# Linear attention: compact decayed queries, and a PSUM bank of level products per head instead of per pair of heads

## The chip, the cores and the metric

The kernel runs on one core of one Trainium2 chip. The metric is the device time of one execution in microseconds (us). Three runs of the kernel before gave a median of 2939.26 us (2933.54 to 2946.39).

## What is computed

The reference is one layer of a streaming encoder over two inputs, a prompt of 2048 tokens and 64 new tokens of a running stream, both 1024 wide. One projection feeds three groups of heads: gated linear attention (4 heads, keys of 64, values of 128), stick-breaking attention (4 heads of 64) and a short gated convolution. Their joined output is projected, added and normed, and a feed-forward part with squared ReLU follows. The change is in the gated linear attention alone, which works in chunks of 64 tokens:

```
b = cumsum(lg)                                   # per head and key channel
att[t, s] = sum_k q[t,k] * k[s,k] * exp(b[t,k] - b[s,k])     for s <= t
o = (q * exp(b)) @ S + att @ v
S = exp(b_last) * S + (k * exp(b_last - b))^T @ v
```

## The kernel before

The program has three phases, each closed by a barrier of all engines: `phase_in` (the input norm, the projection, the convolution), `phase_gla` (the gated linear attention) and `phase_tail` (stick-breaking attention, output projection, feed-forward). The change touches only `phase_gla`.

**Tiling.** Tokens come in four groups of 512 and one of 64 (`GG`), groups in tiles of 128, tiles in chunks of 64. The four heads lie as two pairs: a tile of queries or keys has 128 partitions, where partitions 0 to 63 are the 64 channels of a pair's first head and 64 to 127 those of its second, and an axis of 2 for the pair.

**Levels.** The decay between two tokens of a tile is computed without large exponents, by halving: on a level with half size hs (32, 16, 8, 4, 2, 1) each block of 2·hs tokens is cut in the middle. Keys of the first half are multiplied with the decay up to the cut (L1040), queries of the second half with the decay from the cut on (L1046), and a product of the two gives the attention of later on earlier halves. `level_arg` (VectorE, L1030 and L1031) writes the two exponents' arguments into a buffer `ex` of three slots, ScalarE takes the exponent (L943), `level_mul` (VectorE) multiplies with keys (in place, in `ex`) and queries (into `qb`, which holds only the 256 queries of second halves out of 512 tokens), `level_product` (TensorE, L1143) multiplies the two into the PSUM tile `ps_l`, two banks of 512 columns, and `level_put` copies the valid blocks into `att`: on ScalarE for levels 0 and 1 (L956, one instruction for each block of rows), on VectorE with a mask for levels 2 to 5 (L1074). A seventh step, the diagonal (`li == NL`), multiplies plain keys and queries of one token and head (L1150), with operands of 64 partitions, a bank for each head of the pairs, two tiles at a time.

**Queries with zeros.** Before, `qb` has an axis for the head: `qb[P, EX, 2, 2, 256]`, slot, pair, head, query. The first head's queries stand in partitions 0 to 63 of the first part, the second head's in partitions 64 to 127 of the second; the rest was zeroed once by GpSimd. So one product of all 128 partitions gives both heads of a pair side by side: 128 weight columns (the tile's keys) against 2 x 64 queries, four products (tiles) for each of two banks, one bank per pair. A float32 product shows in the trace as two records of matmul and two of weight load, so a level has 16 records of each.

**Around the levels.** For each tile: `intra` (att times values, L1189), `inter` (queries times state, L1210) and `state` (VectorE, L1093) for each of its chunks, `squares`, `root` and `norm` (the output's norm: ScalarE L972, TensorE L1220, ScalarE L980 and L982, VectorE L1104 and L1107), and for the next tile `turn` (keys turned by TensorE, L1161, copied by ScalarE, L965) and `kv` (L1176).

**Order.** A Python list `order` holds all steps; each engine walks through it and does its part, with semaphores between engines. The steps of group g+1's levels (`ahead`) are spread by weights over the tile steps of group g, from the fourth place on; the first group's stand before everything. Within a group the steps follow as: argument of level li+1, multiplication of level li, copy of level li-1, product of level li. These waits matter:

- a product waits for its level's multiplications (`lev_mul`), and for each bank until the level before has been copied out of that bank;
- a copy waits for the product's end in its own bank (`lev_mm`), so the first bank can be copied while the second is computed;
- the argument of level li waits until the product of level li-3 has read its slot of `ex`;
- `intra` waits for all copies of its group.

SP issues the loads and stores of the phase, and no DMA is changed. ScalarE and VectorE wait at the start for the memsets (`consts_set`): eps and the state on VectorE, `att` on VectorE (L988), `qs` and `qb` on GpSimd (L1225, L1226).

Of the kernel before, what the change touches and what calls it, by code (L numbers as in the profile page):

```python
# [20 lines left out]
P = 128  # L21
# [662 lines left out]
def phase_gla(nc, a, zt_dram, gv_dram, mixt_dram, lasting):  # L684
# [8 lines left out]
    with s:  # L693
# [11 lines left out]
        att = s.sb("att", [P, 2, 2, 4, 2, P])  # L705
        eb = s.sb("eb", [P, 2, 2, 512])

        qb = s.sb("qb", [P, EX, 2, 2, 256])
        qs = s.sb("qs", [P, 2, 2, 2, 512])
        ksf = s.sb("ksf", [P, 2, 2, 512])  # L710
        gg = s.sb("gg", [P, 2, 4, 512])
# [190 lines left out]
        def _(act):  # L902
# [2 lines left out]
                act.dma_start(bg[:], a["b_gate"][0].rearrange("(a p) -> p a", p=P)).then_inc(gate_in, 16)  # L905
            for dst, src in ((starts[:], a["chunk_start"][:, :512]), (masks[:], a["level_masks"]), (ident[:], a["ident"]), (ones[:], a["ones"])):
                act.dma_start(dst, src).then_inc(consts_in, 16)
            act.wait_ge(consts_set, 5)
            act.wait_ge(gate_in, 48)
            for step, *at in order:  # L910
                if step == "gate":
# [11 lines left out]
                elif step == "gate_log":  # L923
                    g = at[0]
                    n = GG[g][1]
                    act.wait_ge(gate_abs, g + 1)
                    act.activation(ga[:, :, :n], ga[:, :, :n], ACT.Exp, scale=-1.0).then_inc(gate_exp, 1)
                    act.wait_ge(gate_exp, g + 1)
                    act.activation(ga[:, :, :n], ga[:, :, :n], ACT.Ln, bias=1.0).then_inc(gate_ln, 1)
                elif step == "gate_sum":  # L930
                    g = at[0]
                    n, q = GG[g][1], g % 2
                    act.wait_ge(cum_done, 2 * (g + 1))
                    if g >= 2:
                        act.wait_ge(st_new, tiles[tiles_before[g - 1]][3][0])
                    act.activation(eb[:, q, :, :n], bc[:, q, :, :n], ACT.Exp, scale=1.0 / TAU).then_inc(eb_done, 1)
                    act.wait_ge(ks_arg, g + 1)
                    act.activation(ksf[:, q, :, :n], ksf[:, q, :, :n], ACT.Exp, scale=1.0 / TAU).then_inc(ks_exp, 1)
                elif step == "level_arg" and at[1] < NL:
                    g, li = at  # L940
                    n, x = GG[g][1], lev_no[(g, li)]
                    act.wait_ge(lev_arg, 2 * (x - g + 1))
                    act.activation(ex[:, x % EX, :, :n], ex[:, x % EX, :, :n], ACT.Exp, scale=1.0 / TAU).then_inc(lev_exp, 1)  # L943
                elif step == "level_put" and at[1] < BY_ROWS:
                    g, li = at
                    n = GG[g][1]
                    b, w, nt, hs = bank_no[(g, li, 0)], min(P, n), max(1, n // P), LEVELS[li]
                    wo = w // 2
                    if g >= 2 and li == 0:
                        act.wait_ge(o_mm, tiles_before[g - 1])  # L950
                    for e in range(2):
                        act.wait_ge(lev_mm, 2 * b + e + 1)
                        dst = att[:, g % 2, e, :nt, :, :w].rearrange("p a h t -> p (a h) t")
                        for x in range(w // (2 * hs)):
                            rows = slice(2 * hs * x, 2 * hs * x + hs)
                            put = act.activation(dst[rows, :, 2 * hs * x + hs:2 * hs * x + 2 * hs],  # L956
                                                 ps_l[rows, e, :2 * nt * wo].rearrange("p (x t) -> p x t", x=2 * nt)[:, :, hs * x:hs * x + hs], ACT.Copy)
                        put.then_inc(put_a, 1)
                elif step == "turn":
                    j = at[0]  # L960
                    m = tiles[j][2]
                    act.wait_ge(k_turned, j + 1)
                    if j >= 2:
                        act.wait_ge(kv_mm, tiles[j - 2][3][-1] + 1)
                    act.activation(kt[:m, j % 2, :], ps_k[:m, 0:256], ACT.Copy).then_inc(k_out, 1)  # L965
                elif step == "squares":
                    j = at[0]
                    m = tiles[j][2]
                    act.wait_ge(o_mm, j + 1)
                    if j:  # L970
                        act.wait_ge(n_mm, j)
                    act.activation(sq[:, :4 * m], ps_o[:, j % 2, :4 * m], ACT.Square).then_inc(sq_done, 1)  # L972
                elif step == "root":

                    j = at[0]
                    m = tiles[j][2]
                    act.wait_ge(n_mm, j + 1)
                    if j:
                        act.wait_ge(o_norm, j)
                    act.activation(rn[:, :4 * m], ps_g[:, :4 * m], ACT.Ln, scale=QSCALE * QSCALE / DV, bias=eps[:, :]).then_inc(n_ln, 1)  # L980
                    act.wait_ge(n_ln, j + 1)
                    act.activation(rn[:, :4 * m], rn[:, :4 * m], ACT.Exp, scale=-0.5).then_inc(n_exp, 1)  # L982

        @block.vector
        def _(dve):
            dve.memset(eps[:], LN_EPS).then_inc(consts_set, 1)
            dve.memset(st[:, 0, :, :], 0.0).then_inc(consts_set, 1)
            dve.memset(att[:], 0.0).then_inc(consts_set, 1)  # L988
            dve.wait_ge(consts_in, 64)
            for step, *at in order:  # L990
                if step == "gate_sum":
                    g = at[0]
# [15 lines left out]
                elif step == "decay":  # L1008
# [3 lines left out]
                    if g >= 2:  # L1012
                        dve.wait_ge(o_mm, tiles_before[g - 1])
                    dve.wait_ge(group_in[q], 48 * (g // 2 + 1))
                    dve.wait_ge(consts_set, 5)
                    for e in range(2):
                        r = slice(64 * e, 64 * e + 64)
                        dve.tensor_tensor(qs[r, q, :, e, :n], eb[r, q, :, :n], gq[r, q, :, :n], ALU.mult).then_inc(qs_done, 1)
# [13 lines left out]
                elif step == "level_mul" and at[1] < NL:  # L1032
# [5 lines left out]
                    k1, _ = halves(gk[:, q], g, hs, n)  # L1038
                    _, q2 = halves(gq[:, q], g, hs, n)
                    dve.tensor_tensor(e1, e1, k1, ALU.mult).then_inc(lev_mul, 1)  # L1040
                    dve.wait_ge(consts_set, 5)
                    if x >= EX:
                        dve.wait_ge(lev_mm, last_bank[lev_by_no[x - EX]])
                    for e in range(2):
                        r = slice(64 * e, 64 * e + 64)
                        dve.tensor_tensor(qb[r, x % EX, :, e, :n // 2].rearrange("p a (b h) -> p a b h", h=hs), e2[r], q2[r], ALU.mult).then_inc(lev_mul, 1)  # L1046
                elif step == "level_put" and at[1] >= BY_ROWS:

                    g, li = at
# [3 lines left out]
                    for (lj, ts) in level_blocks(g):  # L1053
# [3 lines left out]
                        for e in range(2):  # L1057
# [2 lines left out]
                                dve.wait_ge(lev_put, put_no[2 * b - 1][1])  # L1060
                            if li < NL:

                                dst = att[:w, g % 2, e, ts[0]:ts[0] + nt, :, :w].rearrange("p a h t -> p (a h) t")
                                hs, wo = LEVELS[li], w // 2
                                nb = w // (2 * hs)
                                for_pairs = dst.rearrange("p x (b two h) -> p x b two h", two=2, h=hs)[:, :, :, 1, :]
                                data = ps_l[:w, e, :2 * nt * wo].rearrange("p (x b h) -> p x b h", x=2 * nt, h=hs)
                                mk = masks[:w, 64 * li:64 * li + wo].bitcast(I32).rearrange("p (b h) -> p b h", h=hs).unsqueeze(1).to_broadcast([w, 2 * nt, nb, hs])
                            else:

                                for_pairs = att[:w, g % 2, :, ts[0]:ts[0] + nt, e, :w]
                                data = ps_l[:w, e, :2 * nt * w].rearrange("p (x a t) -> p x a t", x=2, a=nt)
                                mk = masks[:w, 64 * NL:64 * NL + w].bitcast(I32).unsqueeze(1).unsqueeze(1).to_broadcast([w, 2, nt, w])
                            dve.copy_predicated(for_pairs, mk, data).then_inc(lev_put, 1)  # L1074
                elif step == "state":
# [2 lines left out]
                    g, i, m, cs = tiles[ct]  # L1078
                    q, end = g % 2, i * P + x * CHUNK + CHUNK - 1
                    dve.wait_ge(kv_mm, c + 1)  # L1080
                    dve.wait_ge(consts_set, 5)
                    if c == FIRST_STREAM:
                        dve.wait_ge(st_in, 16)
                    if c:
# [25 lines left out]
        def _(pe):  # L1110
            pe.wait_ge(gate_in, 48)
            gates_seen = tiles_seen = 0
            for step, *at in order:
# [11 lines left out]
                elif step == "level_product":  # L1125
# [1 line left out]
                    x = lev_no[(g, li)]  # L1127
                    w = min(P, GG[g][1])
                    if li < NL:
                        pe.wait_ge(lev_mul, 3 * (x - g + 1))  # L1130
                    for (lj, ts) in level_blocks(g):
                        if lj != li:
                            continue
# [1 line left out]
                        for e in range(2):  # L1135
                            if b:
                                pe.wait_ge(*put_no[2 * b - 2 + e])
                            for n, t in enumerate(ts):
                                cols = slice(t * P, t * P + w)
                                if li < NL:  # L1140

                                    wo = w // 2
                                    mm = pe.matmul(ps_l[:w, e, n * w:n * w + w], ex[:, x % EX, e, cols], qb[:, x % EX, e, :, t * wo:t * wo + wo],  # L1143
                                                   start=n == 0, stop=n == len(ts) - 1, skip_group_check=True)
                                    continue

                                r = slice(64 * e, 64 * e + 64)
                                for pr in range(2):
                                    at_ = (pr * len(ts) + n) * w
                                    mm = pe.matmul(ps_l[:w, e, at_:at_ + w], gk[r, g % 2, pr, cols], gq[r, g % 2, pr, cols],  # L1150
# [44 lines left out]
                elif step == "inter":  # L1195
# [8 lines left out]
                    elif c:  # L1204
                        pe.wait_ge(st_new, c)
                    else:
                        pe.wait_ge(consts_set, 5)
                    cols = slice(i * P + x * CHUNK, i * P + x * CHUNK + CHUNK)
                    for pr in range(2):
                        mm = pe.matmul(ps_o[:, j % 2, 2 * m * pr:2 * m * pr + 2 * m].rearrange("p (e t) -> p e t", e=2)[:, :, x * CHUNK:x * CHUNK + CHUNK],  # L1210
# [11 lines left out]

        @block.gpsimd
        def _(pool):
            pool.memset(qs[:], 0.0).then_inc(consts_set, 1)  # L1225
            pool.memset(qb[:], 0.0).then_inc(consts_set, 1)  # L1226


def phase_tail(nc, a, zt_dram, mixt_dram, xn_dram, ks_dram, vs_dram, wd_dram, wp_dram, y_tile, lasting):
# [1107 lines left out]
```

## Time and profile before

| | |
|---|---|
| median of three runs | 2939.26 us (2933.54 to 2946.39) |
| profiled execution, its own time | 2947.04 us |
| its span in the trace | 2945.2 us |
| TensorE busy in the span | 2634.0 us, 89% |
| VectorE busy | 1711.7 us, 58% |
| ScalarE busy | 932.2 us, 32% |
| GpSimd busy | 620.3 us, 21% |
| linear attention phase in the span | 654 to 926 us |

The profile is one execution, written down by the chip's profiler. "PE" is TensorE's matmul, "PEld" its weight load, DVE is VectorE, ACT is ScalarE, POOL is GpSimd; SP issues DMAs. L1143 is line 1143 of the kernel. Busy time is the union of an engine's instructions; matmuls are pipelined, so a group's busy time is not the sum of its durations, and a record's duration is longer than the distance to the next. PEclk is the granted clock of TensorE as a share of 2.4 GHz. In a timeline, equal neighbours of one engine are merged (xN), and the bracket tells how long the engine had been idle and what released it.

### The profile page before, as it was taken

The page shows a single profiled execution, that of the slowest core. Times are in us where ns is not written, and L with a number is a line of the kernel's source. Part 1 is how long each engine was busy: PE and PEld are TensorE (multiplying, and loading weights), DVE is VectorE, ACT ScalarE, POOL GpSimd, SP SyncE. Part 2 cuts the span into 40 slices and gives each one's busy share as a digit, 9 for nine tenths or more (in the row PEclk, how much of TensorE's full clock was granted, in tenths as well). Part 3 has the DMA queues.
Part 4 walks back from the last instruction along what each step waited for, and adds up shares of the span by engine and source line. Part 5 has one row for each costly group of instructions (what it writes and reads, how often), then busy time and mean ns, then how long its engine had stood idle before and what let it go on. Part 6 is the DMA issues. An engine that isn't in the chain of part 4 may idle for free.

```text
span 2945.2 us, 37243 instructions
## 1 busy us (share of the span) xinstructions
PE 2634.0 (89%) x13462; PEld 2195.1 (75%) x13462; DVE 1711.7 (58%) x2482; ACT 932.2 (32%) x1816; POOL 620.3 (21%) x617
## 2 busy tenths in 40 slices
PE   6999999975774779999899999989999979999996
PEld 4887777973553568887687878868788767898985
DVE  6676667437784666666566555646656435533334
ACT  3333333313433434443413333322333220221220
POOL 4888788830000110000011000001000001000001
PEclk9999999996787689999999999999999989999998
DMA  7989887851224749898857777755777753767763
GB/s 243 314 298 306 294 293 271 279 176 57 69 65 150 230 158 323 322 342 293 301 175 259 271 288 283 279 206 212 280 292 264 260 197 138 256 243 258 256 245 130
DMA packets 251076, 705.07 MB, mean 239 GB/s; under 512 B 26576, under 2 KB 110640, under 8 KB 202384
## 3 DMA queue, kind: packets, MB, share of 16 engines
q1 hardware_dynamic: 191760, 583.12, 56.1%
q0 software_dynamic: 24560, 88.37, 8.2%
q10 hardware_dynamic: 34576, 31.21, 3.2%
q8 instruction: 110, 1.80, 0.3%
q14 instruction: 70, 0.57, 0.1%
HBM read 541.05 MB, written 161.56 MB: 239 GB/s over the span
## 4 chain that ended last, share of the span: by engine, by line
PE 59%; DVE 3%; issue 3%; DMA 1%; ACT 1%; POOL 1%; SPq 0%; POOLq 0%; DVEq 0%; ACTq 0%
PE p_ps_d L121 18%; PE p_ps_d L122 17%; PE p_ps_d L123 17%; PE p_ps_a L2232 2%; PE p_ps_o L2246 1%; PE p_ps_z L2219 1%; PE p_ps_o L2245 1%; PE p_ps_z L2220 1%; POOL p_rstd L2088 1%; DMA p_kk<-ks_scratch 1%; DVE p_keep L2053 0%; DVE p_xl L1985 0%; DMA p_res<-in_w_out 0%; DVE p_res L1920 0%; DVE p_sl L1998 0%
## 5 line engine op out<-in xcount | busy, mean ns | idle before, releaser
L1920 DVE SCALAR_TENSOR_TENSOR p_res<-p_res,p_ps_d 128x512 f32<-128x512 f32 x508 | 344.0, 684 | 361.3 <-PE p_ps_d L123 357.6
L121 PE MATMUL p_ps_d<-p_xh,p_wp 128*128 128x512 f32 (+1 forms) x1280 | 454.8, 355 | 8.0 <-DVE p_xl L1985 8.0
L122 PE MATMUL p_ps_d<-p_xh,p_wp 128*128 128x512 f32 (+1 forms) x1280 | 453.7, 354 | 0.0
L123 PE MATMUL p_ps_d<-p_xl,p_wp 128*128 128x512 f32 (+1 forms) x1280 | 453.1, 354 | 0.0
L121 PE MATMUL p_ps_d<-p_wp,p_sh 128*128 128x512 f32 x912 | 362.1, 397 | 14.3 <-issue 9.7
L122 PE MATMUL p_ps_d<-p_wp,p_sl 128*128 128x512 f32 x912 | 358.0, 392 | 0.0
L123 PE MATMUL p_ps_d<-p_wp,p_sh 128*128 128x512 f32 x912 | 357.8, 392 | 0.0
L2097 POOL TENSOR_TENSOR p_aw<-p_sg,p_keep 128x512 f32<-128x512 f32 (+2 forms) x84 | 89.6, 1066 | 1240.9 <-DVE p_keep L2053 1240.9
L121 PEld LDWEIGHTS p_ps_d<-p_xh,p_wp 128*128 128x128 f32 x1280 | 242.7, 190 | 38.0 <-DVE p_xl L1985 8.9
L1847 ACT ACTIVATE p_y<-p_ps_d 128x512 f32<-128x512 f32 (+1 forms) x160 | 83.5, 522 | 578.2 <-PE p_ps_d L123 576.8
L123 PEld LDWEIGHTS p_ps_d<-p_xl,p_wp 128*128 128x128 f32 x1280 | 242.7, 190 | 31.2
L122 PEld LDWEIGHTS p_ps_d<-p_xh,p_wp 128*128 128x128 f32 x1280 | 242.5, 189 | 28.6
L490 DVE TENSOR_TENSOR p_wl<-p_wst,p_wh 128x512 fp32r<-128x512 f32 x192 | 210.7, 1131 | 78.8 <-ACT p_wh L385 62.3
L121 PE MATMUL p_ps_m<-p_xh,p_wh 128*128 128x512 f32 (+1 forms) x640 | 229.4, 358 | 3.2 <-DVE p_wl L490 3.2
L2053 DVE TENSOR_TENSOR_SCAN p_keep<-p_tg,p_keep,p_zero 128x513 f32<-128x513 f32 (+1 forms) x100 | 128.4, 1284 | 170.9 <-ACT p_tg L1888 170.8
L122 PE MATMUL p_ps_m<-p_xh,p_wl 128*128 128x512 f32 (+1 forms) x640 | 226.9, 355 | 0.0
L123 PE MATMUL p_ps_m<-p_xl,p_wh 128*128 128x512 f32 (+1 forms) x640 | 226.9, 354 | 0.0
L1888 ACT ACTIVATE p_tg<-p_ps_z 128x512 f32<-128x512 f32 (+5 forms) x168 | 87.4, 520 | 402.2 <-PE p_ps_z L2220 402.1
L121 PEld LDWEIGHTS p_ps_d<-p_wp,p_sh 128*128 128x128 f32 x912 | 173.0, 190 | 54.1 <-issue 18.1
L123 PEld LDWEIGHTS p_ps_d<-p_wp,p_sh 128*128 128x128 f32 x912 | 172.8, 189 | 37.2
L122 PEld LDWEIGHTS p_ps_d<-p_wp,p_sl 128*128 128x128 f32 x912 | 173.2, 190 | 33.7
L385 ACT ACTIVATE p_wh<-p_wst 128x512 fp32r<-128x512 f32 x192 | 116.5, 628 | 229.4 <-DMA p_wst<-in_w_in 217.6
(182 smaller groups left out, 4929.6 us busy)
## 6 DMA issues: line engine op xcount, KB each, us to landing
p_wp<-wd_scratch SPq DMA_DIRECT2D x219, 1024.0 KB, 5.6
p_wp<-wp_scratch SPq DMA_DIRECT2D x120, 1024.0 KB, 6.9
wd_scratch<-p_ppair POOLq DMA_DIRECT2D x120, 512.0 KB, 4.9
wp_scratch<-p_wp SPq DMA_DIRECT2D x40, 1024.0 KB, 5.4
p_wst<-in_w_in SPq DMA_DIRECT2D x128, 256.0 KB, 4.7
p_kk<-ks_scratch SPq DMA_DIRECT2D x84, 256.0 KB, 6.8
p_vv<-vs_scratch SPq DMA_DIRECT2D x84, 256.0 KB, 3.1
p_praw<-in_w_down POOLq DMA_DIRECT2D x32, 512.0 KB, 5.6
```

What stands on the lines that cost most here:

```text
L121: pe.matmul(out, lhs_hi, rhs_hi, start=first, stop=False, skip_group_check=skip)
L122: pe.matmul(out, lhs_lo, rhs_hi, start=False, stop=False, skip_group_check=skip)
L123: return pe.matmul(out, lhs_hi, rhs_lo, start=False, stop=last, skip_group_check=skip)
L385: highs = act.activation(wh[:, gc % 2, k, :], wst[:, w % WSTAGE, :512], ACT.Copy)
L490: lows = dve.tensor_tensor(wl[:, gc % 2, k, :], wst[:, w % WSTAGE, :512], wh[:, gc % 2, k, :].bitcast(F32), ALU.subtract)
L1847: act.activation(y[:, f, o:o + cc], ps_d[:, bank_of[(("up", *at), x)], :cc], ACT.Relu).then_inc(relu_done, 1)
L1888: act.activation(tg[:m, n % SIG, 512 - w:512], ps_z[:m, :w], ACT.Sigmoid, scale=-SCALE).then_inc(sig_done, 1)
L1920: dve.scalar_tensor_tensor(out=acc, in0=acc, scalar=scale, in1=ps_d[:c, bank, :], op0=ALU.mult, op1=ALU.add).then_inc(d_free, 1)
L2053: dve.tensor_tensor_scan(keep[:m, n % KEEP, 512 - w:513][:, ::-1], tg[:m, n % SIG, 512 - w:513][:, ::-1], zero[:m, :].to_broadcast([m, w + ...
L2088: pool.tensor_tensor(rstd[:c, :], veps[:c, :], power[:c, :], ALU.pow).then_inc(rstd_done, 1)
L2097: pool.tensor_tensor(aw[:m, u % AW, i, :w], sg[:m, n % SIG, :w], keep[:m, n % KEEP, 513 - w:513], ALU.mult).then_inc(a_pool, 1)
L2232: mm = pe.transpose(ps_a[:kn, c0:c0 + m], aw[:m, u % AW, i, k0:k0 + kn], ident[:m, :m])
```

## The change

The queries lose the axis for the head: `qb[P, EX, 2, 256]`, slot, pair, query, and one instruction of 128 partitions writes them. There are no zeros any more. Each product takes only one head's 64 partitions of keys and queries, with 128 weight columns and 64 queries; a bank now holds one head of each pair (both pairs, all tiles) instead of both heads of one pair. So there are eight products for each bank and level in place of four. The copies address `att` accordingly: by head of the pair instead of by pair. `att`'s memset goes from VectorE to GpSimd and `qb`'s falls away.

```diff
-        qb = s.sb("qb", [P, EX, 2, 2, 256])
+        qb = s.sb("qb", [P, EX, 2, 256])
...
-            act.wait_ge(consts_set, 5)
+            act.wait_ge(consts_set, 4)
...
-                        dst = att[:, g % 2, e, :nt, :, :w].rearrange("p a h t -> p (a h) t")
+                        dst = att[:, g % 2, :, :nt, e, :w].rearrange("p a n t -> p (a n) t")
...
-            dve.memset(att[:], 0.0).then_inc(consts_set, 1)
             dve.wait_ge(consts_in, 64)
+            dve.wait_ge(consts_set, 4)
...
-                    dve.wait_ge(consts_set, 5)
                     if x >= EX:
                         dve.wait_ge(lev_mm, last_bank[lev_by_no[x - EX]])
-                    for e in range(2):
-                        r = slice(64 * e, 64 * e + 64)
-                        dve.tensor_tensor(qb[r, x % EX, :, e, :n // 2].rearrange("p a (b h) -> p a b h", h=hs), e2[r], q2[r], ALU.mult).then_inc(lev_mul, 1)
+                    dve.tensor_tensor(qb[:, x % EX, :, :n // 2].rearrange("p a (b h) -> p a b h", h=hs), e2, q2, ALU.mult).then_inc(lev_mul, 1)
...
-                                dst = att[:w, g % 2, e, ts[0]:ts[0] + nt, :, :w].rearrange("p a h t -> p (a h) t")
+                                dst = att[:w, g % 2, :, ts[0]:ts[0] + nt, e, :w].rearrange("p a n t -> p (a n) t")
...
-                        pe.wait_ge(lev_mul, 3 * (x - g + 1))
+                        pe.wait_ge(lev_mul, 2 * (x - g + 1))
...
+                            r = slice(64 * e, 64 * e + 64)
...
-                                    mm = pe.matmul(ps_l[:w, e, n * w:n * w + w], ex[:, x % EX, e, cols], qb[:, x % EX, e, :, t * wo:t * wo + wo],
-                                                   start=n == 0, stop=n == len(ts) - 1, skip_group_check=True)
+                                    for pr in range(2):
+                                        at_ = (pr * len(ts) + n) * wo
+                                        mm = pe.matmul(ps_l[:w, e, at_:at_ + wo], ex[r, x % EX, pr, cols], qb[r, x % EX, pr, t * wo:t * wo + wo],
+                                                       start=n + pr == 0, stop=n + pr == len(ts), skip_group_check=True)
...
+            pool.memset(att[:], 0.0).then_inc(consts_set, 1)
             pool.memset(qs[:], 0.0).then_inc(consts_set, 1)
-            pool.memset(qb[:], 0.0).then_inc(consts_set, 1)
```

## Rows read from the trace of the kernel before

**Rows 1.** The page's head: span, and busy time of each engine.

```profile
span 2945.2 us, 37243 instructions
...
PE 2634.0 (89%) x13462; PEld 2195.1 (75%) x13462; DVE 1711.7 (58%) x2482; ACT 932.2 (32%) x1816; POOL 620.3 (21%) x617
```

**Rows 2.** Busy time by stretch: start:end, length, busy us (instructions), clock, DMA.

```profile
core 0: us, PE busy (x) PEld busy (x) DVE busy (x) ACT busy (x) POOL busy (x), PEclk, DMA share, GB/s
654.00:926.00 272.00, 171.18 (x1164) 132.40 (x1164) 201.25 (x348) 106.42 (x188) 6.20 (x3) 0.78 0.23 69
794.50:852.15 57.65, 39.98 (x276) 30.73 (x276) 46.61 (x74) 24.60 (x41) 0.00 (x0) 0.83 0.25 75
749.53:765.01 15.48, 10.89 (x95) 9.46 (x95) 15.26 (x26) 5.27 (x9) 0.00 (x0) 1.00 0.45 134
```

**Rows 3.** Timeline, first half of a period: start, us, engine, line, [idle before].

```profile
794.50 3.78 PE L1143 MATMUL p_ps_l<-p_qb,p_ex 128*128 128x128 f32 x16 [7.24 <-DVE p_qb L1046]
...
798.07 1.91 PE L1220 MATMUL p_ps_g<-p_sq,p_ones 128*128 128x512 f32 x2
...
798.32 0.69 DVE L1030 TENSOR_TENSOR p_ex<-p_bc 128x512 f32<-128x512 f32 x1 [0.63 <-PE p_ps_l L1143]
...
800.73 1.05 ACT L943 ACTIVATE p_ex<-p_ex 128x1024 f32<-128x1024 f32 x1
...
801.81 0.69 DVE L1040 TENSOR_TENSOR p_ex<-p_ex,p_gk 128x512 f32<-128x512 f32 x1 [2.20 <-ACT p_ex L943]
```

**Rows 4.** Timeline, second half of the period before: VectorE's copies, level 5's product.

```profile
752.76 1.31 DVE L1074 COPY_PREDICATED p_att<-p_masks,p_ps_l 128x512 f32<-128x512 int32 x2
...
763.72 2.21 PE L1143 MATMUL p_ps_l<-p_qb,p_ex 128*128 128x128 f32 x16 [1.86 <-DVE p_att L1074]
...
765.01 2.44 DVE L1074 COPY_PREDICATED p_att<-p_masks,p_ps_l 128x512 f32<-128x512 int32 x2
...
768.13 1.33 DVE L1074 COPY_PREDICATED p_att<-p_masks,p_ps_l 128x512 f32<-128x512 int32 x2 [0.69 <-PE p_ps_l L1150]
```

**Rows 5.** Timeline, first group: the pair that writes queries, and its followers.

```profile
683.36 1.40 DVE L1046 TENSOR_TENSOR p_qb<-p_ex,p_gq 64x512 f32<-64x512 f32 x2
...
684.78 0.69 DVE L1030 TENSOR_TENSOR p_ex<-p_bc 128x512 f32<-128x512 f32 x1
...
685.39 0.68 DVE L1031 TENSOR_TENSOR p_ex<-p_bc 128x512 f32<-128x512 f32 x1
```

**Rows 6.** Timeline, last group: a single and a pair.

```profile
901.08 0.22 DVE L1040 TENSOR_TENSOR p_ex<-p_ex,p_gk 128x64 f32<-128x64 f32 x1 [1.59 <-ACT p_ex L943]
...
901.22 0.46 DVE L1046 TENSOR_TENSOR p_qb<-p_ex,p_gq 64x64 f32<-64x64 f32 x2
```

**Rows 7.** TensorE: blocks of records in the timeline; then two half microseconds of one line.

```profile
758.05 2.02 PE L1143 MATMUL p_ps_l<-p_qb,p_ex 128*128 128x128 f32 x16 [1.73 <-DVE p_att L1074]
...
766.94 1.72 PE L1150 MATMUL p_ps_l<-p_gq,p_gk 64*128 64x128 f32 x16
...
768.91 1.76 PE L1150 MATMUL p_ps_l<-p_gq,p_gk 64*128 64x128 f32 x16 [0.26 <-DVE p_att L1074]
...
770.60 0.68 PE L1176 MATMUL p_ps_s<-p_v,p_kt 64*64 64x128 f32 x16
...
916.73 1.10 PE L1189 MATMUL p_ps_o<-p_att,p_v 64*128 64x64 f32 x8
...
758.60:759.10 0.50, 0.50 (x7) 1.00 0.00 0
...
767.50:768.00 0.50, 0.50 (x10) 1.00 0.00 0
```

**Rows 8.** Timeline, the phase's start: memsets and what comes first behind them.

```profile
655.26 3.47 DVE L988 MEMSET p_att<- 128x4096 f32 x1 [0.80 <-issue]
...
657.49 2.65 POOL L1226 MEMSET p_qb<- 128x3072 f32 x1
...
665.01 0.69 ACT L918 ACTIVATE p_gy<-p_ps_g,p_bg 128x512 f32<-128x512 f32 x1 [9.69 <-PE p_ps_g L1123]
...
671.92 1.22 DVE L996 SCALAR_TENSOR_TENSOR p_gy<-p_gy,p_ga 128x1024 f32<-128x1024 f32 x1 [13.19 <-ACT p_ga L929]
```

More of the change, by code:

```diff
@@ L1014, in _ @@
                     dve.wait_ge(group_in[q], 48 * (g // 2 + 1))
-                    dve.wait_ge(consts_set, 5)
+                    dve.wait_ge(consts_set, 4)
                     for e in range(2):
@@ L1040, in _ @@
                     dve.tensor_tensor(e1, e1, k1, ALU.mult).then_inc(lev_mul, 1)
-                    dve.wait_ge(consts_set, 5)
                     if x >= EX:
                         dve.wait_ge(lev_mm, last_bank[lev_by_no[x - EX]])
-                    for e in range(2):
-                        r = slice(64 * e, 64 * e + 64)
-                        dve.tensor_tensor(qb[r, x % EX, :, e, :n // 2].rearrange("p a (b h) -> p a b h", h=hs), e2[r], q2[r], ALU.mult).then_inc(lev_mul, 1)
+                    dve.tensor_tensor(qb[:, x % EX, :, :n // 2].rearrange("p a (b h) -> p a b h", h=hs), e2, q2, ALU.mult).then_inc(lev_mul, 1)
                 elif step == "level_put" and at[1] >= BY_ROWS:
@@ L1080, in _ @@
                     dve.wait_ge(kv_mm, c + 1)
-                    dve.wait_ge(consts_set, 5)
+                    dve.wait_ge(consts_set, 4)
                     if c == FIRST_STREAM:
@@ L1142, in _ @@
                                     wo = w // 2
-                                    mm = pe.matmul(ps_l[:w, e, n * w:n * w + w], ex[:, x % EX, e, cols], qb[:, x % EX, e, :, t * wo:t * wo + wo],
-                                                   start=n == 0, stop=n == len(ts) - 1, skip_group_check=True)
+                                    for pr in range(2):
+                                        at_ = (pr * len(ts) + n) * wo
+                                        mm = pe.matmul(ps_l[:w, e, at_:at_ + wo], ex[r, x % EX, pr, cols], qb[r, x % EX, pr, t * wo:t * wo + wo],
+                                                       start=n + pr == 0, stop=n + pr == len(ts), skip_group_check=True)
                                     continue
-                                r = slice(64 * e, 64 * e + 64)
                                 for pr in range(2):
@@ L1206, in _ @@
                     else:
-                        pe.wait_ge(consts_set, 5)
+                        pe.wait_ge(consts_set, 4)
                     cols = slice(i * P + x * CHUNK, i * P + x * CHUNK + CHUNK)
```

## The prediction

> **What bounds the kernel now.** I read the page's head first: TensorE is busy 89% of the span, VectorE 58% [rows 1]. That is an average over three phases. The change touches only the linear attention, which runs from 654 to 926 us, and there the table by stretch shows the opposite order: VectorE 201 us busy of 272, TensorE 171, ScalarE 106 [rows 2]. Phases end in a barrier, so 272 us is all that can move, and what the phase saves reaches the end one for one. In a steady period, from one group's first level product to the next group's (57.65 us, three of them), VectorE is busy 46.6 us and TensorE 40 us [rows 2]. No engine is full; the phase is a relay, and the question at each level is who arrives last. The timeline answers it in two halves. In the first half of a period TensorE and ScalarE arrive last: the first product, at the lower clock of 1.2 GHz (16 records in 3.78 us, where 2.4 GHz needs 2.02 [rows 7]) behind a pause of 7.24 us, is followed in TensorE's order by the sum of squares and the key turn, and only behind these comes ScalarE's exponent, so that VectorE waits 0.63 and 2.20 us, one piece behind the other [rows 3]. In the second half, levels 3 to 5, VectorE is busy 15.26 of 15.48 us [rows 2].
>
> **The change, part by part.**
>
> *Decayed queries.* Each level now writes them with one instruction over 128 partitions in place of two over 64. The pair of L1046 starts at 683.36 and its follower at 684.78: 1.42 us. Operations of the same 512 columns on 128 partitions follow each other every 0.60 us (684.78, 685.39) and last 0.68 us [rows 5]. The new instruction has the sources of L1046 and the size of L1040, so it costs 0.60 to 0.70 and the level saves 0.72 to 0.82 us; I take 0.75. For 24 levels of the four full groups that is 18.0 us. In the last group, of 64 tokens, a pair takes 0.46 us and a single 0.22 us [rows 6], 6 x 0.24 = 1.4 us. VectorE loses 19.4 us of work. That is the ceiling of the gain.
>
> *Products.* Before, a bank held a pair of heads: four products of 128 rows, 128 weight columns and 128 queries (half of them against zeros), two records each, 16 records for both banks, 2.02 us at full clock, 112 ns apart [rows 7]. After, a bank holds one head of each pair: eight products of 64 rows, 128 weight columns and 64 queries, so 32 records for both. Halving rows and columns does not make a record shorter: the last group's value products already have exactly 64 rows, 128 weight columns and 64 moving columns, and eight of their records take 1.10 us, (1.10 - 0.32)/7 = 0.11 us apart [rows 7]. So a bank's 16 records take 15 x 0.112 + 0.28 + 0.1 for the first = 2.06 us. Both banks one after the other would be 3.8 us. But the two banks now lie on different halves of the rows, as the diagonal's products do already. There, 16 records take 1.72 us rather than 2.02, though the second head's had to wait for VectorE's copy that ended at 767.45 [rows 4, 7]; in the half microsecond behind that copy 10 records are in flight, against 7 for products of full height [rows 7]. So the heads run side by side, and I take 2.06 us for each, the second starting when its own bank is free, some 0.6 us behind the first. The first bank is then ready 0.9 us later than before, the second 0 to 0.65 us later. At 1.2 GHz 16 records side by side take what 16 take now, 3.8 us. Bounds: no lag (second bank at 2.06) and no overlap (3.8).
>
> *Changing between heights.* Between forms of different height TensorE loses about 0.1 us: the diagonal's last block ends at 770.67 and its follower starts at 770.60, 0.07 us before that end, where records of one form lie 0.11 apart and last some 0.3 (2.02 less 15 x 0.112), so that they overlap by 0.2 [rows 7]. Two changes for each product, 24 x 2 x 0.1 = 4.8 us of TensorE, most of it in levels where VectorE is the last; I count 0.5 us on the path (0 to 4.8).
>
> *Copies out of the banks.* Sizes and counts stay. Only the stride of the target doubles, which the diagonal's copy at the same line already has: 1.33 us for two, against 1.31 [rows 4]. Zero, at most 32 x 0.02 = 0.6 us. The waits on the number of multiplications (2 in place of 3) cost nothing.
>
> *Memsets.* att's 3.47 us go from VectorE to GpSimd, in place of the 2.65 us for the old queries; GpSimd then ends at about 661 in place of 660.14 [rows 8]. ScalarE waits for it, but its first operation starts at 665.01, behind the gate product, and VectorE's first real one at 671.92 [rows 8]. Zero, with 4 us of cover.
>
> *What reaches the end.* In a steady period: level 0's saving starts the first product 0.75 us earlier; levels 1 and 2 save 1.5 us that VectorE then waits, because it stands waiting for the exponent already [rows 3]. Product 1 waits for ScalarE's copies, its second head ends 0.65 us later, and behind it stand the tile's att and state products and VectorE's state update; so the 0.75 is eaten. First half: 0. Levels 3 to 5 save 3 x 0.75 = 2.25 us on a VectorE without gaps [rows 2]. At level 5 the copy of the first bank starts 1.3 us behind its product's start (765.01 against 763.72) [rows 4]; it will be 2.1 us, and a second copy follows: 0.8 to 0.9 us lost. Sum -1.35 us, and for three periods -4.1. The first group has no tile work to wait for, but its levels 0 to 2 hang on ScalarE, whose copies now start later, and its last product is cold: of 4.5 us saved I count 1.0 (0 to 4.5). Last group: 0.5 of its 1.4 (0 to 1.4), as its levels stand between tile steps. With +0.5 for changes of height: **-5.1 us**. The sum is made against the profiled execution (span 2945.2 us [rows 1], 1.8 us around it, 2947.04 in all), which is 7.8 us above the median of 2939.26; taken from it the sum gives 2941.9, and taken from the median **2934 us**.
>
> **Rivals.**
> *A. VectorE's whole saving counts.* The wait moves along with it if TensorE's clock stays high in the first half (fewer pauses), which frees the 1.5 us of levels 1 and 2. For it: VectorE has the most work. Against: its waits of 0.63 and 2.20 us [rows 3], which it would reach earlier. Gives up to -19, 2920 us. Chance 0.15.
> *B. The lag is larger.* The second head's 16 records must overtake 16 in the queue; the diagonal shows it for 8. Each product on the path (0, 1, 2, 5) that gets 0.35 us later eats the 1.35 us of a period; with 0.9 us, half a bank, the period loses up to 3.6 and the phase ends 5 to 10 us later: 2944 to 2949. Chance 0.15.
> *C. The slower side: no overlap.* Products take 3.8 us (7.2 cold). On the path of a period: +2.7 (level 0, cold, less its earlier start), +1 each at 1 and 2, +0.9 at 5, -0.75 x 2 for levels 3 and 4, where VectorE's own 3.7 us a level (1.2, 0.6, 0.65, 1.3) nearly cover 3.8: +4.1, for three periods +12.4, first group +5: 2956 us. It decides from 1.8 us a product on; at 0.35 it only cancels the gain. Chance 0.08. The Trainium skill, "TensorE: Matmul & The Clock Gate" (Part 3: Packing small matmuls), says matmuls keep program order in start and end, and only weight loads pass those of other rows. By that rule the second head, 16 records behind, could not begin before the first has started all its own, and the sum would be C's. The diagonal's rows speak against it, 10 records in flight against 7.
> *D. The forecast,* -14 to +1: 0.62.
>
> **Numbers.** About 0.5% (14.7 us) is what a measurement of this kernel can tell from no change. Faster by more: A, with a little of D, 0.16. Slower by more: C, 0.08. The rest, 0.76, within. The range leaves out C and the edge of A: 2921 to 2949.
>
> **What would show it.** Right: L1046 x24 at about 0.69 us, VectorE's busy time in the phase down by 20 to 24 us (the memset included); 32 records for a level, 1.9 to 2.8 us from first start to last end at full clock; the first bank's copy waiting at level 5; VectorE's idle time up by over 10 us; the phase 265 to 269 us. Wrong: products of 3.6 us or more (C), or a phase of 255 us with VectorE's idle time unchanged (A). If the rest of the program moves by more than the phase, it is not this change.

## The result: 3.3% slower

The changed kernel took 3036.31 us (median of 4, 3033.34 to 3040.94) against 2941.43 us for the kernel before beside it: a ratio of 1.0327 with a 95% interval of 1.0303 to 1.0352. Forecast were 2934 us and 2921 to 2949. The profiled execution has a span of 3031.9 us, 86.7 more than before's 2945.2 [rows 1], and the linear attention phase, from its first memset to the next phase's, went from 271.6 to 359.9 us. So the loss of 88 us is all in the phase that was changed; the rest took 2672.0 us against 2673.6. Over all profiled executions of this document that rest varies from 2661 to 2674 us, so a difference of a few us is better read from the phase than from the whole.

First the head of the page of the changed kernel, then its busy time by stretch: the phase, the first 28 us of level products, and 25 us from a steady period (columns as in [rows 2]; numbers in brackets are instructions).

```profile
span 3031.9 us, 38001 instructions
...
PE 2748.1 (91%) x13870; PEld 2301.3 (76%) x13870; DVE 1685.9 (56%) x2451; ACT 933.1 (31%) x1816; POOL 623.3 (21%) x617
```

```profile
650.42:1010.28 359.86, 283.70 (x1572) 237.47 (x1572) 182.52 (x315) 106.80 (x188) 6.95 (x3) 0.58 0.17 53
680.53:708.53 28.00, 28.00 (x169) 28.00 (x169) 15.65 (x24) 7.87 (x16) 0.00 (x0) 0.50 0.00 1
775.00:800.00 25.00, 25.00 (x144) 22.33 (x144) 10.21 (x14) 4.48 (x8) 0.00 (x0) 0.57 0.08 22
```

The same two stretches of the kernel before, the phase and the first 28 us of its level products:

```profile
654.04:925.67 271.63, 171.18 (x1164) 132.40 (x1164) 201.16 (x346) 106.42 (x188) 6.10 (x3) 0.78 0.23 69
684.81:712.81 28.00, 20.82 (x130) 18.95 (x130) 24.91 (x35) 8.04 (x17) 0.00 (x0) 0.83 0.00 1
```

VectorE has 18.6 us less work (201.2 to 182.5), somewhat less than the 20 to 24 that were forecast with the memset. By line, writing the queries fell from 35.4 to 17.7 us and `att`'s memset took 3.5 us with it, but the copies behind the products rose from 41.1 to 43.4 us. One copy takes the same time as before; two of them just no longer run partly into each other. First before, then the changed kernel (line, count, busy us, mean ns, idle time before them and what ended it):

```profile
L1074 DVE COPY_PREDICATED p_att<-p_masks,p_ps_l 128x512 f32<-128x512 int32 x48 | 41.1, 910 | 8.4 <-PE p_ps_l L1150 5.9 <-PE p_ps_l L1143 2.0
...
L1071 DVE COPY_PREDICATED p_att<-p_masks,p_ps_l 128x512 f32<-128x512 int32 x48 | 43.4, 908 | 65.0 <-PE p_ps_l L1143 48.8 <-PE p_ps_l L1149 15.8
```

TensorE, which was not the bound, now has 283.7 us of work instead of 171.2. The number behind POOL's is the granted clock: in the first 28 us TensorE is busy 28.00 of 28.00 us and its clock is granted at 0.50 (1.2 GHz) throughout, where the kernel before was busy 20.82 and had 0.83.

The timeline of a period's first half, TensorE and VectorE, answers to [rows 3]; two later products and a copy answer to [rows 4]:

```profile
745.14 6.29 PE L1143 MATMUL p_ps_l<-p_qb,p_ex 64*128 64x64 f32 x32 [6.48 <-DVE p_qb L1043]
...
751.36 2.07 PE L1219 MATMUL p_ps_g<-p_sq,p_ones 128*128 128x512 f32 x2
...
751.47 0.69 DVE L1030 TENSOR_TENSOR p_ex<-p_bc 128x512 f32<-128x512 f32 x1 [3.98 <-PE p_ps_l L1143]
...
755.26 0.69 DVE L1040 TENSOR_TENSOR p_ex<-p_ex,p_gk 128x512 f32<-128x512 f32 x1 [2.50 <-ACT p_ex L943]
...
756.01 6.26 PE L1143 MATMUL p_ps_l<-p_qb,p_ex 64*128 64x64 f32 x32 [0.48 <-DVE p_ex L1040]
...
779.33 0.71 DVE L1071 COPY_PREDICATED p_att<-p_masks,p_ps_l 128x512 f32<-128x512 int32 x1 [4.85 <-PE p_ps_l L1143]
...
792.41 3.74 PE L1143 MATMUL p_ps_l<-p_qb,p_ex 64*128 64x64 f32 x32
```

In the three steady periods 15 of the 18 products take 6.3 us and three 3.4 to 3.8, where the clock is full (792.41); the first group's six take 32.5 us together, less than six times 6.3, because there the heads overlap from one product to the next as well. The second half of a period, where VectorE had been busy without a gap [rows 2], now has waits of 4.85 us for TensorE at one copy. Two things are in the 6.3 us: a pace of 213 ns a record (half clock), and 28 steps of that pace instead of 16. The steps show in the records in flight in three microseconds of the product at 756.01, by its start, its middle and its end (TensorE alone: length, busy, records, clock):

```profile
756.30:757.30 1.00, 1.00 (x6) 0.50 0.00 0
758.60:759.60 1.00, 1.00 (x10) 0.50 0.00 0
760.60:761.60 1.00, 1.00 (x6) 0.50 1.09 258
```

Only in the middle do both heads run. From the start times in the trace, the second head's first record starts 2.59 us behind the product's first, 6 ns behind the first head's 13th. So it passed three records, no more: the first head's last four run beside the second head's first four. That leaves 32 - 4 = 28 steps, and 27 x 0.213 and the last record's 0.42 are 6.2 us.

### The profile page after: what moved, and what is told of

Its sections match the earlier page's. It is cut to its first block, busy times and chain, and to the rows that moved or that the text cites. A ratio compares the mean times of both kernels' runs of the same rounds, so it can differ in the third digit from the quotient of the medians.

```text
span 3031.9 us, 38001 instructions
## 1 busy us (share of the span) xinstructions
PE 2748.1 (91%) x13870; PEld 2301.3 (76%) x13870; DVE 1685.9 (56%) x2451; ACT 933.1 (31%) x1816; POOL 623.3 (21%) x617
## 4 chain that ended last, share of the span: by engine, by line
PE 57%; DVE 3%; issue 3%; DMA 1%; ACT 1%; POOL 1%; SPq 0%; POOLq 0%; ACTq 0%; DVEq 0%
PE p_ps_d L121 17%; PE p_ps_d L122 17%; PE p_ps_d L123 17%; PE p_ps_a L2231 2%; PE p_ps_z L2218 1%; PE p_ps_o L2245 1%; PE p_ps_o L2244 1%; PE p_ps_z L2219 1%; POOL p_rstd L2087 1%; DMA p_kk<-ks_scratch 1%; DVE p_keep L2052 0%; DVE p_xl L1984 0%; DMA p_res<-in_w_out 0%; DMA p_wp<-wp_scratch 0%; DVE p_res L1919 0%
```

## The experiments

Twelve kernels ran. The theory after the result had two causes, the overlap that is only four records deep and the clock; the rivals were that one of them was only a result of the other, and that TensorE's 64-row records cost something else.

**The heads in turns.** TensorE issues one product of the first head, one of the second, and so on. In return, each copy waits for both banks and each product for both copies.

```diff
-                            dve.wait_ge(lev_mm, 2 * b + e + 1)
+                            dve.wait_ge(lev_mm, 2 * b + (2 if li < NL else e + 1))
...
+                        if li < NL and len(ts) > 1:
+                            wo = w // 2
+                            if b:
+                                for e in range(2):
+                                    pe.wait_ge(*put_no[2 * b - 2 + e])
+                            todo = [(n, t, pr) for n, t in enumerate(ts) for pr in range(2)]
+                            for k in range(0, len(todo), 1):
+                                for e in range(2):
+                                    r = slice(64 * e, 64 * e + 64)
+                                    for n, t, pr in todo[k:k + 1]:
...
```

> The changed kernel, but TensorE issues the two heads' products of a level in turns, one product each, and each copy waits for both banks. Theory 1 (the second head can only pass about four records of the first in the queue, and TensorE's clock follows how many of the array's rows are at work): 32 records start in 16 steps, the clock rises in mid-period as before, a product takes about 2.1 us at 2.4 GHz and 3.8 us at 1.2 GHz, 2930 to 2950 us. Theory 2 (the clock follows the moving columns streamed per time, which 64-column records halve): 16 steps as well, but the clock stays at 1.2 GHz, products 3.8 us, 2970 to 2990 us. Theory 3 (no order makes the heads overlap more than by four records): 6.3 us a product and about 3036 us.

2971.25 us, ratio 1.0105 (1.0065 to 1.0145). All products take 16 steps; the clock comes late. Three products in the timeline, then a microsecond of the first one, TensorE alone, and the first 28 us of products:

```profile
744.65 3.68 PE L1143 MATMUL p_ps_l<-p_qb,p_ex 64*128 64x64 f32 x32 [6.99 <-DVE p_qb L1043]
...
753.69 3.68 PE L1143 MATMUL p_ps_l<-p_qb,p_ex 64*128 64x64 f32 x32 [1.27 <-ACT p_att L956]
...
760.16 2.00 PE L1143 MATMUL p_ps_l<-p_qb,p_ex 64*128 64x64 f32 x32
```

```profile
744.90:745.90 1.00, 1.00 (x12) 0.50 0.00 0
...
679.55:707.55 28.00, 18.39 (x160) 17.57 (x160) 15.94 (x24) 7.87 (x16) 0.00 (x0) 0.50 0.00 1
```

Twelve records are in flight where the changed kernel had six. So order alone gives back 65 of the 95 us, and theory 3 falls. The time is in the range of theory 2, but the clock was between the other two: granted 0.50 in the first 28 us, with TensorE busy for 18.39, and full from the third product of a period on.

**Turns of two and of four products,** the same edit with the step 1 replaced by 2 and by 4: how far a head can pass the other.

> The heads in turns of two products (four records) each. If the second head can pass about four records of the first, the heads overlap nearly fully, 17 to 18 steps a product: 3.9 to 4.1 us at 1.2 GHz, about 2.1 at 2.4, time near that of turns of one product, 2960 to 2985. If the window is one product only: 6 us and 3020 or more.

> The heads in turns of four products (eight records) each. If the second head can pass four records, half of each turn overlaps: some 20 to 24 steps a product, 4.5 to 5.3 us at 1.2 GHz, 2985 to 3015 us. If the window is eight or more: 16 to 18 steps and 2960 to 2985.

One execution each: 2966.28 and 3006.36 us. Turns of two cost nothing against turns of one (3.70 and 2.05 us a product). Turns of four take 4.7 us at 1.2 GHz:

```profile
750.72 4.71 PE L1143 MATMUL p_ps_l<-p_qb,p_ex 64*128 64x64 f32 x32 [6.99 <-DVE p_qb L1043]
```

Three changes of head with four records side by side at each would make 32 - 12 = 20 steps, and the start times in the trace show 20 (19 x 0.213 and the last record's 0.42 are 4.5 us; the rest is about 0.06 us at each change and at the first record). With turns of one and of two products the start times show 16 steps. The depth of four is shown from both sides.

**Higher and wider records.** Two kernels keep the changed kernel's order. One takes all 128 rows (`ex[:, ...]`, `qb[:, ...]` in place of `ex[r, ...]`, `qb[r, ...]`), the other 128 moving columns.

> The changed kernel with products of all 128 rows in place of 64 (each bank gets the sum over both heads, so the attention of the levels is not the reference's): 32 records of 128 rows, 128 weight columns, 64 moving columns, which cannot overlap. Theory 1 (rows at work set the clock): the clock rises, products take about 3.8 us at 2.4 GHz, 2960 to 2990 us in spite of the lost overlap. Theory 2 (moving columns set it): the clock stays at 1.2 GHz, products 7.2 us, 3055 to 3085 us.

> The changed kernel with 128 moving columns in place of 64 in each product (taken from the decayed keys, results lie over each other, so the attention of the levels is not the reference's): 32 records of 64 rows, 128 weight columns, 128 moving columns, at the pace the weight loads set already. Theory 1 (rows at work): the clock stays low as in the changed kernel, 3030 to 3045 us. Theory 2 (moving columns): the clock rises, products about 3.4 us, 2970 to 3000 us.

3007.3 us and 2985.82 us (two runs each; ratios 1.023 and 1.0157). The tall records overlap nowhere and take 7.09 us a product at 1.2 GHz, 3.7 where the clock is full, and the kernel still is 29 us faster than the changed one. The wide ones overlap by four, as in the changed kernel, and are 50 us faster. Neither theory of what the clock follows held alone: with either change the granted clock of the phase rose, from 0.58 to 0.67 and 0.72:

```profile
652.85:995.03 342.18, 262.24 (x1572) 226.50 (x1572) 181.46 (x315) 107.04 (x188) 6.95 (x2) 0.67 0.18 55
```

```profile
648.23:959.88 311.65, 233.94 (x1572) 194.23 (x1572) 180.30 (x315) 106.41 (x188) 6.96 (x3) 0.72 0.20 61
```

In both, the first 28 us stayed at 0.50 although TensorE was busy for all of them. What exactly grants the clock is left open; TensorE's pauses don't explain it.

**Zeros behind the queries.** The wide form with the right result: `qb` gets 128 columns for each tile, of which the last 64 stay zero, and each product but a bank's last streams all 128.

```diff
-        qb = s.sb("qb", [P, EX, 2, 256])
+        qb = s.sb("qb", [P, EX, 2, 4, 128])
...
+                                        wide = wo if n + pr == len(ts) or len(ts) == 1 else 2 * wo
+                                        mm = pe.matmul(ps_l[:w, e, at_:at_ + wide], ex[r, x % EX, pr, cols], qb[r, x % EX, pr, t, :wide],
```

> The changed kernel in its own order of products, only that each product but a bank's last streams 64 columns of zeros behind its 64 queries. Same records, same pace of a record by the weight loads, same overlap of four records. If the low clock is a cause of its own: products 3.5 us at 2.4 GHz in most of the second halves, 2970 to 2990 us, some 50 us under the changed kernel. If the clock follows from the order of the heads: 3030 to 3040.

3000.1 us, ratio 1.0207 (1.0184 to 1.023): 36 us better than the changed kernel for streaming zeros. A record keeps its pace, and from the third product of a period on most take 3.44 us. One of three periods stayed at 1.2 GHz nearly to its end, hence less than the 50 us expected. So the clock is a cause of its own.

```profile
757.26 6.37 PE L1146 MATMUL p_ps_l<-p_qb,p_ex 64*128 64x128 f32 x32 [0.48 <-DVE p_ex L1040]
...
766.42 4.03 PE L1146 MATMUL p_ps_l<-p_qb,p_ex 64*128 64x128 f32 x32
...
773.06 3.44 PE L1146 MATMUL p_ps_l<-p_qb,p_ex 64*128 64x128 f32 x32
```

**Both mended: turns and zeros.**

> The heads in turns, and each product streams its 64 queries and 64 columns of zeros (but the last of a bank); the weight loads set the pace of a record already, so a record takes the same time. VectorE writes the queries with one instruction of 128 partitions. Theory (what keeps the clock at 1.2 GHz is how much of the array is at work per time, rows times moving columns, and zeros count): the clock in the phase is that of the kernel before (granted 0.78), products take 2.0 us at 2.4 GHz, and only the forecast's steps are left: 2928 to 2940 us, 0 to 10 us under the kernel before. If zeros don't count or only the height of one product does: the clock and the time of the heads in turns without padding, 2960 to 2980 us.

2956.16 us, ratio 1.0049 (1.003 to 1.0068). The clock is that of before (0.78), products take 2.0 us, 3.5 to 3.7 when cold, and yet the kernel is 15 us over the kernel before (10.4 in the phase, 282.07 against 271.63), where 0 to 10 under it were expected.

```profile
652.63:934.70 282.07, 178.40 (x1572) 141.63 (x1572) 179.77 (x315) 107.04 (x188) 9.56 (x4) 0.78 0.22 67
...
682.68:710.68 28.00, 17.03 (x192) 16.25 (x192) 16.90 (x25) 7.87 (x16) 0.00 (x0) 0.76 0.00 1
```

**The relay between the banks.** Before, TensorE fills a bank while the other is copied; turns give that up. The kernel before, with its own products, but both banks waited for together:

```diff
-                        act.wait_ge(lev_mm, 2 * b + e + 1)
+                        act.wait_ge(lev_mm, 2 * b + 2)
...
-                            dve.wait_ge(lev_mm, 2 * b + e + 1)
+                            dve.wait_ge(lev_mm, 2 * b + (2 if li < NL else e + 1))
...
-                                pe.wait_ge(*put_no[2 * b - 2 + e])
+                                pe.wait_ge(*put_no[2 * b - 2 + (1 if li < NL else e)])
```

> The kernel before, but each bank's copy waits for both banks of the product and each product for the copies of both banks: what the heads in turns need, with the products of before. The padded heads in turns have VectorE's saving (17 us with one write) and the clock of before, and still are 15 us over the kernel before: if the lost relay between the two banks is the reason, this costs 15 to 32 us, 2956 to 2973. If something else in the 64-row products costs it (changes of height, the longer cold products): 0 to 8 us, 2941 to 2949.

2964.04 us, ratio 1.0075 (1.0045 to 1.0105), 22 us over the kernel before: waiting for both banks costs about that. A part of it is the clock: the second product of each period is cold here too (3.5 to 3.65 us), as with the turns, where the kernel before takes 2.02, and the granted clock of the phase is 0.74.

```profile
652.83:949.32 296.49, 184.81 (x1164) 146.47 (x1164) 201.81 (x346) 107.15 (x188) 6.10 (x3) 0.74 0.21 64
```

Together with VectorE's saving (one write, below) this accounts for the padded turns. In the phases, 24.9 us of waiting less 13.9 of saving are 11.0, and measured are 10.4. In the medians, 22 less 17 are 5 of 15, a gap within the intervals of the three. As far as one profiled execution of each can tell, nothing is left for the changes of height to explain.

**Relay, overlap and clock together.** Padded products in turns, but the first head leads by as many products as the copy of its bank takes, and the second starts when its own bank is free; copies wait for their own bank.

```diff
+                            lead = (1, 3, 5, 3, 3, 5)[li]
+                            todo = [(n, t, pr) for n, t in enumerate(ts) for pr in range(2)]
+                            turns = [(k - lead * e, e) for k in range(len(todo) + lead) for e in range(2) if 0 <= k - lead * e < len(todo)]
+                            for k, e in turns:
+                                n, t, pr = todo[k]
+                                if b and not k:
+                                    pe.wait_ge(*put_no[2 * b - 2 + e])
```

> The padded products in turns, with the relay between the banks kept: the first head leads by 1 to 5 products (by the length of the copies), the second starts as soon as its own bank is copied, each copy waits for its own bank alone. This is what the forecast assumed of the changed kernel. If the changed kernel's loss is only the missing overlap and the low clock: VectorE's 17 us less some us for the later first bank, 2925 to 2938 us. If 64-row products cost more by themselves: 2942 to 2956.

2943.25 us, ratio 1.0008 (0.9994 to 1.0022): the kernel before's time, with products of 2.55 to 3.05 us from first start to last end at full clock.

```profile
652.00:923.25 271.25, 185.71 (x1572) 149.02 (x1572) 178.95 (x315) 106.51 (x188) 9.55 (x4) 0.80 0.23 70
```

```profile
748.25 3.00 PE L1146 MATMUL p_ps_l<-p_qb,p_ex 64*128 64x128 f32 x32
```

All of the 95 us is back, by the order of TensorE's products and the zeros behind the queries alone. Nothing is gained over before, though, and of the two expectations the second came true: 64-row products cost more by themselves. The same saving with before's products gives a phase of 257.73 us (one write, below), so these products cost 13.5 us more than before's, and VectorE's saving pays for them. They end later (2.55 to 3.05 us against 2.0), and the second of a period is cold twice (4.32 and 4.01 us); how the 13.5 us divide was not measured.

**VectorE's part and TensorE's part alone.** One kernel is the changed one with two writes of 64 partitions, the other is the kernel before with one write of 128 (`qb[:, x % EX, :, 0, ...]` from `e2` and `q2`).

> The changed kernel with its products, but the compact queries written in two instructions of 64 partitions, as before the change: the products alone. If TensorE is last at every level of the changed kernel, VectorE's 18 us of saving are all waiting time, and this takes the changed kernel's time plus 0 to 3 us, 3036 to 3040. If the saving reaches the end there too, 3050 to 3056.

> The kernel before, with its products of 128 rows and 128 moving columns, but the queries of both heads written by one instruction of 128 partitions into the first head's columns (so the attention of the levels is not the reference's): VectorE's saving alone. By the forecast's account, in which about a quarter of 19 us reaches the end: 3 to 8 us under the kernel before. If VectorE's whole saving counts: 17 to 20 us under. If none: the same.

3035.63 us (ratio 1.0337, 1.0295 to 1.0378) and 2924.97 us (ratio 0.994, 0.9923 to 0.9958). In the changed kernel no part of VectorE's saving shows in the medians. The whole of it, for which 3050 to 3056 us were expected, lies just outside the interval of the first ratio (12 us to either side), but a part does not: the phases are 359.86 us with one write and 366.79 with two, with the few products at full clock in other places. That TensorE is last at most of these levels shows in the 48.8 us that the copies wait for its level products, where before they waited 2.0. With before's products the saving is worth 17 us by the medians (12 to 23 by the interval) and 13.9 in the phase, of VectorE's 19.4. First two writes, then one write:

```profile
646.11:1012.90 366.79, 292.82 (x1572) 243.57 (x1572) 201.13 (x345) 105.95 (x188) 6.95 (x3) 0.57 0.17 52
...
651.99:909.72 257.73, 165.12 (x1164) 128.14 (x1164) 181.81 (x316) 106.72 (x188) 6.10 (x2) 0.80 0.24 73
```

**The saving by another way.** Since the products of before should stay, GpSimd wrote the second head's queries beside VectorE.

```diff
+                    pool.wait_ge(lev_exp, x - g + 1)
...
+                    pool.tensor_tensor(qb[64:128, x % EX, :, 1, :n // 2].rearrange("p a (b h) -> p a b h", h=hs), e2[64:128], q2[64:128], ALU.mult).then_inc(lev_mul_b, 1)
```

> The kernel before with its products; VectorE writes only the first head's queries, GpSimd (idle in this phase) the second head's, beside it. VectorE's work falls by 0.7 us a level as in the run with one write, TensorE's products keep their form. If GpSimd's half takes under about 1.3 us (a GpSimd operation of 128x512 takes 1.07 us on the page) and is not last: 10 to 17 us under the kernel before, 2925 to 2932 us. If GpSimd and VectorE slow each other down or GpSimd's half is last at each level: 0 to 10 us over it.

2942.51 us, ratio 1.0003 (0.9986 to 1.0019): no gain, at the lower edge of the second expectation. The groups of the phase by line and shape say why:

```profile
L1239 POOL TENSOR_TENSOR p_qb<-p_ex,p_gq 64x512 f32<-64x512 f32 x24 | 47.3, 1979 | 164.6 <-ACT p_ex L944 155.1 <-issue 9.5
...
L1045 DVE TENSOR_TENSOR p_qb<-p_ex,p_gq 64x512 f32<-64x512 f32 x24 | 20.5, 852 | 0.0
```

GpSimd needs 1.98 us on average for its half, and VectorE's own goes from 0.68 to 0.85 us on average. Both averages hide two cases. One instruction of each period takes GpSimd 5.22 us, while VectorE works without a pause (two take 6.46 us together), and the first product waits for it; the others take 1.25 to 1.73 us. And VectorE's own takes 0.67 us in 20 cases and 1.74 in four, beside one of GpSimd's of about 1.7. No version with the reference's result beats the kernel before.

## Why the prediction was wrong

**Products: the overlap was mis-sized.** "So the heads run side by side ... the second starting when its own bank is free, some 0.6 us behind the first." It starts 2.6 us behind at 1.2 GHz (13 records of 213 ns), 1.39 us at 2.4 GHz. The diagonal's rows did show an overlap, but of 8 records by 8, where the second head began (767.50) just behind VectorE's copy (767.45), when by the start times in the trace the first had only three records not yet started. That is just the depth that the changed kernel's products show. Nothing in those rows spoke for passing 16, and rival B named this gap and then gave it 0.9 us. The Trainium skill's rule, "TensorE: Matmul & The Clock Gate" (Part 3: Packing small matmuls), that matmuls keep program order, was turned down because of those rows; the runs stand between the two. The heads do run beside each other, 10 records in flight against 6, but only by four. In the sum this is the term of the second bank's end: counted were 0 to 0.65 us later than before, and at full clock the last record ends 3.4 to 3.8 us behind the first start instead of 2.02. For a head 16 records long the rule's sum was much nearer than mine.

**The clock: the sum took it over from before.** Each duration at 2.4 GHz rested on the clock of a period before. The changed products keep TensorE busy without a pause and still have 1.2 GHz most of the time (0.58 against 0.78 in the phase). Rival C had the right side and almost the right number of steps, but priced most products at 3.8 us; they took 6.3, and so it said 2956 where 3036 came. The two multiply, so their shares don't add up: the clock mended alone (zeros) gives 36 us, the order alone 65, both together 80 (turns and zeros). Both runs with turns also pay for waiting for both banks; without that, both together give 93 (the leading head).

**VectorE's saving: too little, and beside the point.** The forecast let about a quarter of 19 us reach the end, and for the saving alone 3 to 8 us were expected; it is 17 (one write), 13.9 of them in the phase. Rival A came near in size for this part, but without its condition, a clock that stays high: the first product is still cold, 3.78 us. The phase shows where the terms were too small. A period gets shorter by 2.45 us from level 3's product to level 5's (counted 2.25) and by 1.6 from level 5's product to the next first one (counted 0.75), the first group by 2.5 (counted 1.0). The forecast's zero for the first half stands: from the first product to level 3's it is 16.5 us on average before and 16.7 with one write. In the changed kernel none of the saving shows in the medians: two writes or one, 3036.

**What held.** L1043 runs 24 times at 683 ns, a copy takes 908 ns on average against 910, and memsets cost nothing: GpSimd ends them at 657.4 and VectorE's first real operation starts at 668.36. 16 steps of a bank take 2.0 us at full clock, said were 2.06. And with overlap, clock and relay restored (the leading head), the phase takes 271.25 us against 271.6. The forecast gave 266.5 for such a kernel, but that it comes within 5 us is in the main luck: VectorE's saving was larger than its terms (13.9 us), the 64-row products cost more than its terms (13.5 us), and the two errors cancel. The changed kernel itself never ran that way. The changes of height, put at 0 to 4.8 us, were not measured alone.

## What to carry to other kernels

Halving the rows and the moving columns of a matmul gained nothing by itself here: a record with 128 weight columns kept its pace of 112 ns at full clock and 213 at half, with 64 rows or 128 and with 64 moving columns or 128, so two half-height matmuls cost two full ones, unless their row halves really run side by side. Here that worked only a few records deep, so issue the two halves in turns of one or two products, and look at the records in flight rather than at the existence of an overlap. And before TensorE's times are carried over to a new shape, ask which granted clock they had: here 15 of the 18 products in steady periods had half of it, which no duration of the old trace shows. Last, two errors that cancel look like a good forecast: one kernel with each side of a change alone shows them.

## What was not expected of the hardware

- TensorE busy 28.00 of 28.00 us with a granted clock of 0.50, while the kernel before, busy 20.82 of 28, was granted 0.83. Streaming 64 columns of zeros more with each product made the kernel 36 us faster.
- A head's records passed only three of the other row half's that had not started: products of 28, 20 and 16 steps with turns of eight, four and one product.
- Waiting for both banks instead of one costs 22 us (0.75%) over 24 levels, about 0.9 us a level, though nothing is computed more. A part of it is a product of each period that falls to the lower clock.
